# Gate matrix of an expert layer: begun earlier, with more of the projections placed inside it, and two token groups to one product

## The reference, cut to what matters

```
q      = t @ peer_wq                      # 8 heads, 2 halves of 128
scores = q halves against 2 x 128 keys    # top 16 of each half, then top 16 of 256 sums
gate   = softmax(best 16) per head
out    = sum over picks of gate * gelu(t . expert_down[pick]) * expert_up[pick]
```

## Time and profile before

| | before |
|---|---|
| median of 3 runs | 3194.93 us (3193.82 to 3196.19) |
| the profiled execution, its own time | 3199.72 us |
| its span | 3197.9 us |
| TensorE busy | 2961.2 us, 93% |
| VectorE busy | 2312.2 us, 72% |
| ScalarE busy | 1481.0 us, 46% |
| GpSimd busy | 463.6 us, 14% |
| granted TensorE clock, mean | 0.965 |

### The profile page before, as it was taken

One profiled execution on the slowest core, in us unless ns is written; L12 is line 12 of the kernel. 1 busy time (PEld: TensorE's weight loads), 2 busy tenths in 40 slices (PEclk: granted clock), 3 DMA queues, 4 the chain that ended last, 5 costly groups with the idle time before them and its releaser, 6 DMA issues. The chain is left out here.

```text
span 3197.9 us, 48903 instructions
## 1 busy us (share of the span) xinstructions
PE 2961.2 (93%) x19366; PEld 2709.6 (85%) x19366; DVE 2312.2 (72%) x4093; ACT 1481.0 (46%) x2301; POOL 463.6 (14%) x258
## 2 busy tenths in 40 slices
PE   6899998999999898899789999998799989999998
PEld 5788887878888787899789988887699879998887
DVE  4868996686899766793986677777589496556665
ACT  3344333434433344445654445554444575444554
POOL 0100000010000002598000000001279600000000
PEclk8999999999999998999999999999799999999999
DMA  6434554543455452455137677773245414555564
GB/s 196 158 126 165 198 198 151 191 169 128 163 204 198 151 197 87 158 179 181 51 115 240 221 247 240 266 278 124 93 156 182 145 47 147 184 181 194 192 195 160
DMA packets 125975, 547.96 MB, mean 171 GB/s; under 512 B 13715, under 2 KB 17972, under 8 KB 101300
## 3 DMA queue, kind: packets, MB, share of 16 engines
q1 hardware_dynamic: 125604, 544.30, 49.5%
q10 hardware_dynamic: 144, 0.52, 0.0%
HBM read 538.48 MB, written 6.29 MB: 170 GB/s over the span
## 5 line engine op out<-in xcount | busy, mean ns | idle before, releaser
L1978 PE MATMUL e_ps<-k_hhi,q_hi 128*128 128x256 f32 x2304 | 657.6, 285 | 0.0
L1978 PE MATMUL e_ps<-k_hlo,q_hi 128*128 128x256 f32 x2304 | 653.2, 284 | 0.0
L1978 PE MATMUL e_ps<-k_hhi,q_lo 128*128 128x256 f32 x2304 | 653.1, 283 | 0.0
L2258 DVE TENSOR_TENSOR q_lo<-q_raw,q_hi 128x1024 fp32r<-128x1024 f32 x394 | 482.7, 1225 | 184.7 <-ACT q_hi L2067 183.5
L2067 ACT ACTIVATE q_hi<-q_raw 128x1024 fp32r<-128x1024 f32 x538 | 563.8, 1048 | 3.9 <-DMA q_raw<-up 2.4
L738 DVE TENSOR_TENSOR k_wlo<-k_raw,k_whi 128x2048 fp32r<-128x2048 f32 x158 | 360.7, 2289 | 168.8 <-ACT k_whi L565 168.7
L1978 PEld LDWEIGHTS e_ps<-k_hhi,q_hi 128*128 128x128 f32 x2304 | 444.3, 193 | 0.3 <-DVE k_hlo L2285 0.2
L1978 PEld LDWEIGHTS e_ps<-k_hlo,q_hi 128*128 128x128 f32 x2304 | 444.0, 193 | 0.0
L1978 PEld LDWEIGHTS e_ps<-k_hhi,q_lo 128*128 128x128 f32 x2304 | 443.4, 192 | 0.0
L565 ACT ACTIVATE k_whi<-k_raw 128x2048 fp32r<-128x2048 f32 x158 | 300.9, 1910 | 255.1 <-DMA k_raw<-ws 90.5
L1959 POOL TENSOR_TENSOR q_lo<-q_raw,q_hi 128x1024 fp32r<-128x1024 f32 x144 | 370.6, 2585 | 79.9 <-ACT q_hi L2067 79.6
(11 more groups left out here) (352 smaller groups left out, 5464.6 us busy)
## 6 DMA issues: line engine op xcount, KB each, us to landing
k_raw<-ws SPq DMA_DIRECT2D x180, 1024.0 KB, 4.8
q_raw<-down SPq DMA_DIRECT2D x288, 512.0 KB, 3.5
q_raw<-up SPq DMA_DIRECT2D x256, 512.0 KB, 4.2
k_x<-ada SPq DMA_DIRECT2D x48, 512.0 KB, 3.8
e_ada<-ada SPq DMA_DIRECT2D x48, 512.0 KB, 4.9
out<-k_x SPq DMA_DIRECT2D x3, 1024.0 KB, 4.2
k_x<-out SPq DMA_DIRECT2D x3, 1024.0 KB, 7.3
k_x<-x SPq DMA_DIRECT2D x2, 1024.0 KB, 5.9
```

What stands on the lines that cost most here:

```text
L1978: last = nc.tensor.matmul(psD(n), w, h, start=kt == 0 and i == 0, stop=kt == KT - 1 and i == 2)
L2258: V.tensor_tensor(lo[:, i % RING, :], raw[:, i % RING, :], hi[:, i % RING, :].bitcast(F32), ALU.subtract).then_inc(S["lo_dve"], 1)
```

## The change

The gate matrix begins behind 42 rows and not 56, and 37 units lie between its groups and not 11. Two groups (a pair p, 8 tokens) share one product on VectorE and one copy on ScalarE; the bank pair is then 2 of the 4 banks. B becomes a ring of 11 slots: a staged row k is cut at token CUT[k]. Its gelu of tokens before CUT goes into the ring and is multiplied into A when the pair that ends at CUT is done (`staged(p)`, a product of CUT[k] elements), and the gelu of the tokens from CUT on goes straight into A, where the later pairs' product takes it up (so the product of pair p has `rows_in_a(p)` rows, 42 to 76). VectorE's `rest` stands one group closer behind its unit (g - 3, was g - 4). The 48 modulation loads are spread over 164 units, from unit 103.

```diff
-FIRST = 56
-STAGED = 11
+FIRST = 42
+STAGED = 37
+PAIRS = GROUPS // 2
+SIDES = 11
+STAGED_IN = [g for g in range(GROUPS) if staged_after(g) is not None]
+CUT_PAIR = [min(PAIRS, (g + 4) // 2) for g in STAGED_IN]
+CUT = [2 * GROUP * p for p in CUT_PAIR]
+def rows_in_a(p):
+    return FIRST + sum(c <= p for c in CUT_PAIR)
+ADA_SPAN = NU - 5 - ADA_UNIT
-    a = k * MODS // 176
+    a = k * MODS // ADA_SPAN
-    B = pb("e_b", [P, STAGED, T])
+    B = pb("e_b", [P, SIDES, T])
-        psW = lambda g: ps[:, 4 + g % 4, :].rearrange("p (k n) -> p n k", k=GROUP)
+        psW = lambda p: ps[:, 4 + 2 * (p % 2):6 + 2 * (p % 2), :].rearrange("p b (k n) -> p n (b k)", k=GROUP)
...
SP, ahead of unit ADA_UNIT
-                        sp.wait_ge(S["staged_mult"], 1)
+                        sp.wait_ge(S["staged_mult"], STAGED)
...
PE, gates(g)
-                        pe.wait_ge(S["w_read_act"], g - 3)
+                        pe.wait_ge(S["w_read_act"], (g - 4) // 2 + 1)
...
ACT, take(n) of a staged row
-                        ins = nc.scalar.activation(B[:, x - FIRST, :], psD(n), ACT.Gelu)
+                        k = x - FIRST
+                        if k >= SIDES:
+                            act.wait_ge(S["staged_mult"], k - SIDES + 1)
+                        ins = nc.scalar.activation(B[:, k % SIDES, 0:CUT[k]], psD(n)[:, 0:CUT[k]], ACT.Gelu)
+                        if CUT[k] < T:
+                            ins.then_inc(S["b_part"], 1)
+                            ins = nc.scalar.activation(A[:, x, CUT[k]:T], psD(n)[:, CUT[k]:T], ACT.Gelu)
-                def to_a(g):
-                    act.wait_ge(S["w_read_dve"], g + 1)
-                    nc.scalar.activation(A[:, FIRST:NE, g * GROUP:(g + 1) * GROUP], psW(g)[:, FIRST:NE, :], ACT.Copy).then_inc(S["w_read_act"], 1)
+                def to_a(p):
+                    act.wait_ge(S["w_read_dve"], p + 1)
+                    n = rows_in_a(p)
+                    nc.scalar.activation(A[:, n:NE, p * 2 * GROUP:(p + 1) * 2 * GROUP], psW(p)[:, n:NE, :], ACT.Copy).then_inc(S["w_read_act"], 1)
...
ACT, loop over g
-                    to_a(g)
+                    if g % 2:
+                        to_a(g // 2)
...
DVE
+                def into_a(p):
+                    dve.wait_ge(S["w_mm"], 2 * p + 2)
+                    n = rows_in_a(p)
+                    dve.wait_ge(S["psd_read"], PQ + n)
+                    a = A[:, 0:n, p * 2 * GROUP:(p + 1) * 2 * GROUP]
+                    V.tensor_tensor(a, psW(p)[:, 0:n, :], a, ALU.mult).then_inc(S["w_read_dve"], 1)
+                def staged(p):
+                    for k in range(STAGED):
+                        if CUT_PAIR[k] == p:
+                            dve.wait_ge(S["w_read_act"], p)
+                            dve.wait_ge(S["psd_read"], PQ + FIRST + k + 1)
+                            a = A[:, FIRST + k, 0:CUT[k]]
+                            V.tensor_tensor(a, a, B[:, k % SIDES, 0:CUT[k]], ALU.mult).then_inc(S["staged_mult"], 1)
...
DVE, loop over g
-                    if g >= 2:
-                        into_a(g - 2)
-                    n = staged_after(g - 4) if g >= 4 else None
+                    if g >= 3 and g % 2:
+                        into_a((g - 3) // 2)
+                        staged((g - 3) // 2)
+                    n = staged_after(g - 3) if g >= 3 else None
...
DVE, behind the loop
-                dve.wait_ge(S["w_read_act"], GROUPS)
-                a = A[:, FIRST:FIRST + STAGED, :]
-                V.tensor_tensor(a, a, B[:, :, :], ALU.mult).then_inc(S["staged_mult"], 1)
+                staged(PAIRS - 1)
+                staged(PAIRS)
```

More of the change, by code:

```diff
@@ L1814, in staged_after @@
     return PQ + FIRST + n - 1 if n > g * STAGED // GROUPS else None
+STAGED_IN = [g for g in range(GROUPS) if staged_after(g) is not None]
[3 more added lines that the diff above has]
+    return FIRST + sum(c <= p for c in CUT_PAIR)
 ADA_UNIT = PQ + FIRST + STAGED + 8
+ADA_SPAN = NU - 5 - ADA_UNIT
 def next_mod(i):
     k = i - ADA_UNIT
-    a = k * MODS // 176
-    return a if 0 <= a < MODS and (k == 0 or (k - 1) * MODS // 176 < a) else None
+    a = k * MODS // ADA_SPAN
+    return a if 0 <= a < MODS and (k == 0 or (k - 1) * MODS // ADA_SPAN < a) else None
 NEXT_LOADS = [ND + 84 + 9 * k for k in range(4)]
@@ L1894, in peer @@
             dve_step t_sub t_exp iv_ready picks_mm picks_copied hot1_ready hot2_ready hot1_act dist_ready neg_ready w_mm w_read_dve w_read_act
-            staged_mult weighted g_hi_ready g_lo_ready gate_mm gate_ready prod_done x_done out_x in_crow in_ada ada_done""".split()
+            staged_mult b_part weighted g_hi_ready g_lo_ready gate_mm gate_ready prod_done x_done out_x in_crow in_ada ada_done""".split()
         S = {n: cx.enter_context(nc.semaphore("e_" + n + str(l))) for n in names}
@@ L2054, in _ @@
                 last.then_inc(S["gate_mm"], 1)
-                pe.wait_ge(S["w_read_act"], GROUPS)
+                pe.wait_ge(S["w_read_act"], PAIRS)
                 for x in range(NE):
@@ L2115, in weighted_head @@
                     if x < FIRST:
-                        act.wait_ge(S["w_read_dve"], GROUPS)
+                        act.wait_ge(S["w_read_dve"], PAIRS)
                     elif x < FIRST + STAGED:
-                        act.wait_ge(S["staged_mult"], 1)
+                        act.wait_ge(S["staged_mult"], x - FIRST + 1)
                     else:
@@ L2306, in _ @@
                     gated(g)
-                    if g >= 2:
-                        into_a(g - 2)
-                    n = staged_after(g - 4) if g >= 4 else None
+                    if g >= 3 and g % 2:
+                        into_a((g - 3) // 2)
+                        staged((g - 3) // 2)
+                    n = staged_after(g - 3) if g >= 3 else None
                     if n is not None:
                         rest(n + RING)
-                into_a(GROUPS - 2)
-                into_a(GROUPS - 1)
-                for g in range(GROUPS - 4, GROUPS):
+                into_a(PAIRS - 1)
+                for g in range(GROUPS - 3, GROUPS):
                     n = staged_after(g)
```

## The result

The changed kernel takes 3202.19 us (median of 16 runs, 3197.99 to 3207.71), the kernel before 3194.3 us beside it (16 runs, 3182.45 to 3199.57). The ratio is 1.0028, 95% interval 1.0019 to 1.0038: slower by 0.28%, some 8 us. The profiled execution has a span of 3205.6 us against 3197.9, so 7.7 us more. The predicted time was 3202.

What follows compares the result with a forecast made beforehand. TensorE bounds nearly throughout, but inside the gate matrix it waits for VectorE's one-hot rows. To a median of 3194.9 us the phases of both layers add 4.6 and the exp 2.4, giving 3202 us, range 3188 to 3214.

Steps and rivals of the forecast that it cites:

- VectorE's rest would stand for ScalarE: Inside the gate matrix, VectorE's low piece would wait for ScalarE's high piece, near 50 us per layer.
- E pairs: Pairs of groups with a unit behind the even group only, predicted to take 6.53 us each.
- The length of a pair: Inside the gate matrix, from one pair's product on VectorE to the next: 6.53, 6.00 or 7.67 us by where units stand.
- The second gelu: On ScalarE, the extra gelu of a staged unit's take would add 0.08 us.
- B pair: A pair of groups with a unit behind both its groups, predicted to take 7.67 us.
- The phase: From the picks' transposes to ScalarE's last staged take: 210.0 us; net of units moved in, +2.3 us per layer.
- The exp: Ahead of the gate matrix, the exp 14 units earlier would stall TensorE 2.4 us in the second layer.
- The "nothing" for the first layer: The earlier exp would cost nothing there: table load ends at 1468.8 us, the subtraction at 1468.9.
- The table load ahead of the wait: ScalarE would load the exp's table before waiting for the subtraction; behind the wait, all would be 1.3 us later.
- The sums hold: Rival: VectorE's waits in the gate matrix are covered, TensorE bounds the phase at 171.5 us; 3125 us in all, chance 0.07.
- The second gelu's full cost: Rival: the extra gelu on ScalarE costs 0.17 us, not 0.08; 3207 us, up to 3214, chance 0.22.
- the lower clock: Rival: gaps drop TensorE's granted clock below 0.80 in the phase; at 0.7, 3262 us, chance 0.04.

Runs made afterwards that it cites:

- r1: The changed kernel with only VectorE's rest moved back by one group, behind g - 4: 3126.07 us, 0.9786 of the kernel before.
- r2: The changed kernel with the unit's take and head moved ahead of the pair's copy on ScalarE: 3147.79 us, 0.9857 of the kernel before.
- r4: The kernel before with only VectorE's rest moved behind g - 3 instead of g - 4: 3234.11 us, ratio 1.0123.
- r10: The kernel of r1 timed once more in a later session: 3129.60 us, 0.9794 of the kernel before.
- r6: The changed kernel with only the exp two units later: 3202.71 us, 1.0029 of the kernel before.

## Why the prediction was right, point by point

- **That VectorE's rest would stand for ScalarE.** Right and shown: 47.6 us of wait in the layer, some 50 expected; it goes with r1 and for E pairs alone with r2, and comes into the kernel before with r4.
- **The length of a pair.** 6.53, 6.00 and 7.67 us predicted, 6.5, 5.94 and 7.64 measured. The second gelu cost 0.04 to 0.05 us where I took 0.08. The 0.14 us estimated from the Trainium skill (VectorE: DVE Perf Modes, section The TRN2 errata) did not show in the distance between starts: most of it overlaps. The 7.6 us that I gave TensorE in a B pair were the miscount named under r2; it did no harm, since VectorE's 7.67 set the pair either way.
- **The phase.** 210.0 us predicted, 209.4 and 209.6 measured. Against each layer's own phase before, the exchange is +0.4 us in the first layer and +3.1 in the second, 3.5 in both for 4.6 predicted. TensorE stands idle for 30.8 and 31.2 us of the two phases, against 27.6 and 27.7 before; the rest of the 45 us that it loses to its own 164.8 goes mainly to the lower clock. Its waits named after VectorE's one-hot rows, which were to stay, rose on the weight load (16.9 us before, 33.5 now).
- **The exp.** The stall was 2.5 us for 2.4 predicted, and take(54) started at 2486.68 for 2486.4. What I had not counted is the 1.3 us that the unit behind it took longer. With the 0.16 us by which two units otherwise overlap that is 4.0 us, and 3.5 + 4.0 = 7.5 of the 7.7 us by which the span grew. The "nothing" for the first layer held in this trace, but on a margin of 0.1 us: in the traces of r1 and r10, where the subtraction ends 2.6 to 2.8 us later, the stall is there in the first layer too.
- **The table load ahead of the wait.** Right: it starts at 2480.70, the wait lies behind it.
- **The rivals.** "The sums hold" is false for this order and true with r1. The second gelu's full cost and the lower clock did not come: the granted clock of the stretch stayed at 0.94.
- **The size.** Some 8 us of 3194 by the medians, 7.0 predicted; the interval, 0.19 to 0.38%, leaves no change out, but not by much. That the sum of two small terms comes this near is partly luck: one was 1.1 us too large, the other 1.6 too small.

## What to carry to other kernels

Before believing busy sums, write the engines' orders side by side and follow one item from engine to engine: an instruction that waits for something queued behind the answer to the instruction just ahead of it turns two engines into one. The wait is the length of the chain through the other engine less the work that lies between the two in the queue. One place more can decide about the whole rewrite: here 3202 to 3126 us by a single index. Then look at which engine the sums name, and fill that one's last gaps. And count what a change costs in every layer or pass that it touches: the later exp won 3.5 us in one layer and lost as much over both.

## What the runs showed of the hardware

A short stall of TensorE cost more than its own length in one place and not in another. r1 has one of 2.50 us in the first layer and one of 2.54 us in the second. From the first matmul behind the stall to the transposes, the same 24 matmuls in both:
```profile
1474.61:1477.59 2.98, 2.98 (x25) 2.98 (x26) 0.00 (x0) 0.00 (x0) 2.98 (x2) 1.00 0.56 176
2451.24:2455.45 4.21, 4.21 (x25) 4.21 (x25) 0.00 (x0) 0.00 (x0) 4.21 (x2) 0.66 0.62 179
```
Behind the first the granted clock stayed at 1.00, behind the second it was 0.66 and the unit took 1.2 us longer. What makes the difference is not known. In r6, after 5.1 us without work, the first two groups took 3.41 us up to the unit behind them, where two take 1.71 later on; the granted clock from 2495 to 2503 us was 0.61.

A gelu of 64 to 96 elements moved ScalarE's next start by only 0.10 to 0.13 us. Three one-hot rows on VectorE take 0.85 us inside the phase, but 3.00 and 3.67 us at its start beside GpSimd's low pieces (the changed kernel and r6).
